# Output projections of a two-block fp32 kernel: raw weights requested during the attentions, low halves on VectorE, waits by chunk

## The reference

```python
# first block: forgetting attention and sliding-window attention, each 8 heads of 64
y = jnp.concatenate([oa * silu(za), ob * silu(zb)], axis=-1) @ w_out[l]      # 2048x1024 @ 1024x1024
x = x + gate[:, None, :] * rms_norm(y, g_post[l])
# second block: sparse latent attention a (8 heads of 64) and a recurrence r (width 512)
a = a * jax.nn.silu(gate_a)
r = rms_norm_2(r, hgrn_norm_g[l]).reshape(B, E, HGRN_WIDTH) * jax.nn.silu(gate_h)
y = jnp.concatenate([a, r], axis=-1) @ w_out[l]
h = layer_norm(DN_ALPHA * h + y, ln_g[l], ln_b[l])
```

## Time and profile before

| | us |
|---|---|
| median of 3 runs (3675.43 to 3689.69) | 3686.92 |
| profiled execution | 3693.26 |
| its span | 3691.6 |
| TensorE busy (share of the span) | 3301.4 (89%) |
| VectorE busy | 2017.7 (55%) |
| ScalarE busy | 1407.1 (38%) |
| GpSimd busy | 928.1 (25%) |

### The profile page before, as it was taken

One profiled execution on the slowest core, in us unless ns is written; L12 is line 12 of the kernel. 1 busy time (PEld: TensorE's weight loads), 2 busy tenths in 40 slices (PEclk: granted clock), 3 DMA queues, 4 the chain that ended last, 5 costly groups with the idle time before them and its releaser, 6 DMA issues. The chain is left out here.

```text
span 3691.6 us, 43885 instructions
## 1 busy us (share of the span) xinstructions
PE 3301.4 (89%) x15793; PEld 2518.3 (68%) x15840; DVE 2017.7 (55%) x3687; ACT 1407.1 (38%) x2381; POOL 928.1 (25%) x850
## 2 busy tenths in 40 slices
PE   3899999899999996995789999997995999999698
PEld 3799888656666664874567887886773666666387
DVE  5211011366666666332289999965672555555366
ACT  4100001144444444111157999232553333333344
POOL 0111111355454461001321223534232112111100
PEclk9999999899999998997899999998997999999899
DMA  5231224565454422435211335454135324222343
GB/s 200 72 103 62 94 83 122 134 140 128 106 128 106 103 70 100 137 119 213 70 44 49 87 109 177 132 156 165 50 112 158 97 66 93 59 56 59 107 150 128
DMA packets 331914, 400.83 MB, mean 109 GB/s; under 512 B 100324, under 2 KB 249188, under 8 KB 319124
## 3 DMA queue, kind: packets, MB, share of 16 engines
q1 hardware_dynamic: 257624, 282.31, 27.4%
q10 hardware_dynamic: 67488, 78.03, 6.9%
q0 software_dynamic: 6592, 37.75, 3.6%
HBM read 265.39 MB, written 132.62 MB: 108 GB/s over the span
## 5 line engine op out<-in xcount | busy, mean ns | idle before, releaser
L2218 PE MATMUL f_pO<-f_PT,f_vv 128*128 128x512 f32 (+3 forms) x944 | 383.1, 488 | 22.3 <-ACT f_PT L2248 22.3
L2310 DVE TENSOR_REDUCE f_mxc<-f_pM 128x1 f32<-128x512 f32 (+2 forms) x448 | 240.1, 541 | 226.7 <-PE f_pM L2142 129.0
L2248 ACT ACTIVATE f_PT<-f_pS 128x512 f32<-128x512 f32 (+3 forms) x472 | 221.4, 472 | 354.7 <-PE f_pS L2181 175.5
L2315 DVE CUSTOM_DVE_ANT_0 n_junk<-n_pM,n_chosen 128x512 bf16<-128x512 f32 (+4 forms) x352 | 200.2, 571 | 274.2 <-PE n_pM L2148 138.7
L2660 PE MATMUL cbank<-hT_high,cw_hi 128*128 128x512 f32 x800 | 316.6, 396 | 31.1 <-POOL cw_lo L2613 25.4
L2850 DVE TENSOR_SCALAR_CACHE_REDUCE sharedI<-xI,TI 128x768 bf16<-128x768 f32 (+10 forms) x276 | 339.6, 1297 | 5.4 <-DVE TI L2855 5.2
L571 PE MATMUL p_bank<-hT_high,p_w_hi 128*128 128x512 f32 (+1 forms) x768 | 304.9, 397 | 31.9 <-POOL p_w_lo L537 26.3
L2248 ACT ACTIVATE n_PT<-n_pS 128x512 f32<-128x512 f32 (+4 forms) x352 | 177.4, 504 | 390.9 <-PE n_pS L2198 320.1
L2660 PE MATMUL cbank<-hT_low,cw_hi 128*128 128x512 f32 x800 | 313.7, 392 | 0.0
L2660 PE MATMUL cbank<-hT_high,cw_lo 128*128 128x512 f32 x800 | 313.6, 392 | 0.0
L2218 PE MATMUL n_pO<-n_PT,n_vv 128*128 128x512 f32 (+4 forms) x704 | 305.6, 515 | 3.9 <-issue 1.3
(11 more groups left out here) (419 smaller groups left out, 7454.9 us busy)
## 6 DMA issues: line engine op xcount, KB each, us to landing
cw_raw<-in_w_in_dram SPq DMA_DIRECT2D x50, 512.0 KB, 4.6
f_zz<-scratch_z ACTq DMA_DIRECT2D x128, 128.0 KB, 2.9
p_w_raw<-in_w_in_dram SPq DMA_DIRECT2D x23, 512.0 KB, 3.7
scratch_z<-p_stage ACTq DMA_DIRECT2D x32, 256.0 KB, 2.4
scratch_qk_high<-p_stage ACTq DMA_DIRECT2D x32, 256.0 KB, 2.6
scratch_qk_low<-p_stage_low ACTq DMA_DIRECT2D x32, 256.0 KB, 3.2
f_vv<-scratch_vf SPq DMA_DIRECT2D x16, 512.0 KB, 14.4
f_rq<-scratch_qkb POOLq DMA_DIRECT2D x32, 256.0 KB, 6.7
```

The source lines that it names most:

```text
L2218: pe.matmul(pO[:, B % 2, c0:c1], lhsT=vv[0:nk, b, kt, :], rhs=PT[0:nk, u % PR, c0:c1], start=(kt == 0 and not heads[h].local), stop=(heads ...
L2248: act.activation(PT[0:nk, u % PR, c0:c1], pS[0:nk, u % SR, c0:c1], ACT.Exp, scale=0.125).then_inc(s_ex, 1)
L2310: v.tensor_reduce(to, pM[:, n % 2, 0:wd], AX.X, ALU.max).then_inc(s_mx, 1)
L2315: v.tensor_tensor_reduce(junk[:, n % 2, 0:wd], pM[:, n % 2, 0:wd], chosen[:, at:at + wd], 1.0, 3.0 * NEG, ALU.add, ALU.max, accum_out=to). ...
```

## The change

Three edits, in both output stages.

1. A buffer `lent` lives across an attention and the output stage behind it (eight chunks in the first, four in the second). In the attention `cosT`, `sinT`, `rqs`, `rks` ("f_") or `rq` ("n_") are slices of it. Behind the store of the last head's first block SyncE waits until all heads are split (`s_part`) and asks for the raw weights into `lent`, one transfer for two chunks. In o1 that is all of them; in o2 chunks 0 to 3, and GpSimd asks for 4 to 7 in the stage, as before.
2. VectorE subtracts for all eight chunks. ScalarE and VectorE prepare three (`FEW`), run the phases of the turns -3 to -1, and then prepare the other five; SyncE asks for `gain` and `offset` at that same point.
3. TensorE waits for the low parts chunk by chunk inside the first half of tile 0.

```diff
+        MORE = DC - lent.shape[1]
+        more = m.sb(n_("wraw"), [P, MORE, D]) if MORE else None
...
+        AHEAD, BEHIND, FEW = 3, 1, 3
+        def skeleton(phases, between=None):
...
+            turns(range(-AHEAD, 0))
+            if between is not None:
+                between()
+            turns(range(0, NT + BEHIND))
+        def wraw(k):
+            return lent[:, k, :] if k < DC - MORE else more[:, k - (DC - MORE), :]
...
         def _(gp):
-            for k in range(0, DC, 2):
-                gp.dma_start(wraw[:, k:k + 2, :], w_out[0, k * P:(k + 2) * P, :].rearrange("(k p) n -> p k n", p=P)
-                             ).then_inc(s_w[k // 2], 16)
-            split_low(gp, 1)
+            for k in range(DC - MORE, DC, 2):
+                gp.dma_start(more[:, k - (DC - MORE):k - (DC - MORE) + 2, :],
+                             w_out[0, k * P:(k + 2) * P, :].rearrange("(k p) n -> p k n", p=P)).then_inc(s_w[k // 2], 16)
...
                     for k in range(DC):
+                        if n == 0 and z == 0:
+                            pe.wait_ge(s_wl, k + 1)
...
-            for z in range(2):
-                pe.wait_ge(s_wl[z], DC // 2)
             skeleton(((0, multiply),))
...
+            def weights_high(ks):
+                for k in ks:
+                    act.wait_ge(s_w[k // 2], 16)
+                    act.activation(w_hi[:, k, :], wraw(k), ACT.Copy).then_inc(s_wh, 1)
+            weights_high(range(FEW))
...
-            split_low(v, 0)
+            def weights_low(ks):
+                for k in ks:
+                    v.wait_ge(s_wh, k + 1)
+                    v.tensor_tensor(w_lo[:, k, :], wraw(k), w_hi[:, k, :].bitcast(F32), ALU.subtract).then_inc(s_wl, 1)
+            weights_low(range(FEW))
...
# stage_attend, SyncE, in the loop over blocks
+                if j == 0 and h == NH - 1:
+                    sp.wait_ge(s_part, 2 * (NH if rel is not None else len(local_no)))
+                    for to, src, loaded in ahead:
+                        sp.dma_start(to, src).then_inc(loaded, 16)
```

More of the change, by code:

```diff
@@ L748, with stage_out @@
 DN_ALPHA = 2.0 ** 0.25
-def stage_out(nc, used, tag, gated_T, part, gates, w_out, rows_in, rows_out, gate_row=None, ln=None):
+def stage_out(nc, used, tag, gated_T, part, gates, w_out, rows_in, rows_out, lent, s_lent, gate_row=None, ln=None):
     HW = D // 2
@@ L774, in stage_out @@
         pY = m.ps(n_("pY"), [P, 2, D])
[L776 to L777 removed]
+        s_w = s_lent + [m.sem(n_(f"w_loaded{i}")) for i in range(MORE // 2)]
+        s_wh, s_wl = m.sem(n_("w_high")), m.sem(n_("w_low"))
         s_c = m.sem(n_("vectors_loaded"))
@@ L807, in _, with load_vectors @@
         def _(sp):
-            if ln:
-                for dst, src in ((gain, ln[0]), (offset, ln[1])):
-                    sp.dma_start(dst[:], src.to_broadcast([P, D])).then_inc(s_c, 16)
+            def load_vectors():
+                if ln:
+                    for dst, src in ((gain, ln[0]), (offset, ln[1])):
+                        sp.dma_start(dst[:], src.to_broadcast([P, D])).then_inc(s_c, 16)
             def load_parts(n, b, r):
@@ L897, in finish @@
                 act.activation(std[:, b:b + 1], var[:, b:b + 1], ACT.Sqrt).then_inc(s_std, 1)
-            skeleton(((1, high), (-1, finish)) + (((2, gate),) if part is not None else ()))
+            skeleton(((1, high), (-1, finish)) + (((2, gate),) if part is not None else ()), lambda: weights_high(range(FEW, DC)))
         @block.vector
@@ L929, in finish @@
                 one = slice(b, b + 1)
+                if ln and n == 0:
+                    v.wait_ge(s_c, 32)
                 v.wait_ge(s_st[b], r * 16)
@@ L954, in finish @@
                     v.tensor_tensor(tt[:, b, :], tt[:, b, :], xg[:, b, :], ALU.add).then_inc(s_res[b], 1)
-            if ln:
-                v.wait_ge(s_c, 32)
-            skeleton(((1, low), (-1, finish)) + (((2, gate),) if part is not None else ()))
+            skeleton(((1, low), (-1, finish)) + (((2, gate),) if part is not None else ()), lambda: weights_low(range(FEW, DC)))
 def stage_turn(nc, used, rows, meta, blocks, hT_meta, HT):
@@ L2914, in scratch, with lent_weights @@
         return nc.dram_tensor("scratch_" + name, shape, dt, kind="Internal").ap()
+    def lent_weights(w, to, sems):
+        return [(to[:, 2 * i:2 * i + 2, :], w[0, 2 * i * P:(2 * i + 2) * P, :].rearrange("(k p) n -> p k n", p=P), sem)
+                for i, sem in enumerate(sems)]
     HALF = SCRATCH_ROW
@@ L2958, in build_program @@
         heads += [local(H - 2), local(H - 1)]
-        stage_attend(nc, used, "f_", heads, 3, turns=turns, sinks=sinks)
-        stage_out(nc, used, "o1_", GT, None, None, w_out, x[0], X1, gate_row=gate_row)
+        m = Memory(nc, first, used)
+        lent, s_lent = m.sb("lent1", [P, DC, D]), [m.sem(f"o1_w_lent{i}") for i in range(DC // 2)]
+        stage_attend(nc, used, "f_", heads, 3, lent, lent_weights(w_out, lent, s_lent), turns=turns, sinks=sinks)
+        stage_out(nc, used, "o1_", GT, None, None, w_out, x[0], X1, lent, s_lent, gate_row=gate_row)
     clear(nc, used)
@@ L3003, in latent @@
                     k=[rows_of(t, h) for t in KTs])
-    stage_attend(nc, used, "n_", [latent(h) for h in range(H)], 2, rel=(MK, MKT, BV, BVT))
-    stage_out(nc, used, "o2_", GA2, RRT, GHT, w_out_2, X1, out[0], ln=(ln_g, ln_b))
+    with ExitStack() as last:
+        m = Memory(nc, last, used)
+        lent, s_lent = m.sb("lent2", [P, DC // 2, D]), [m.sem(f"o2_w_lent{i}") for i in range(DC // 4)]
+        stage_attend(nc, used, "n_", [latent(h) for h in range(H)], 2, lent, lent_weights(w_out_2, lent, s_lent),
+                     rel=(MK, MKT, BV, BVT))
+        stage_out(nc, used, "o2_", GA2, RRT, GHT, w_out_2, X1, out[0], lent, s_lent, ln=(ln_g, ln_b))
 INPUTS = ["x", "c", "positions", "w_ada", "b_ada", "g_pre", "w_in", "b_fgate", "sinks", "w_out", "g_post",
```

22 lines of the change are left out of this document (5 added, 17 removed).

## The result

| | before | changed |
|---|---|---|
| median, us | 3686.92 (3675.43 to 3689.69) | 3659.60 (3656.68 to 3664.95) |
| profiled execution (span) | 3693.26 (3691.6) | 3664.95 (3663.2) |
| TensorE idle before the two first matmuls | 32.7 + 34.0 | 14.5 + 23.8 |

The ratio is 0.9934, with a 95% interval of 0.9915 to 0.9952: 27.3 us faster, 18 to 31 by the interval. The forecast was 3659.

The account below looks back on a forecast made before the run. TensorE bounds both output stages behind holes of 32.75 and 33.97 us before their first matmuls. Gains of 16.2 (18.4 - 2.2) in o1 and 12.0 in o2 sum to 28.2 us, from 3686.92 to 3659; range 3646 to 3673.

Parts of the forecast that it names:

- The start of o1: First output stage: first matmul 6.7 us behind SyncE's first transfer instead of 25.1, a gain of 18.4 us.
- The end of the attention: Before o1: VectorE's last product waits for a store queued behind the early weights, costing 2.2 us, ends 0 and 8.5.
- The gate load's own term: Last attention block: ScalarE's gate load delayed 1.3 to 2.6 us by the weights, beside the store's 2.2.
- 5.2 us bound from the 7.9 us row: Upper delay of the last gate load, from loads landing in 7.9 to 8.4 us beside GpSimd's raw query loads.
- the rule that the prediction quoted: DMA engines take packets from queues in turn: each gate-load packet waits for one weight packet, 1.3 us in all.
- The start of o2: Second output stage: turned part lands at S + 11.1, first matmul at S + 13.9 instead of 26.7; gain 12.0 after waits.
- The cover of the other five chunks: In o1 the last five subtractions hide under the first tile's matmuls; without that cover they would cost 6.3 us.
- The chunk waits in o2: First tile of o2: TensorE waits some 0.8 us for chunks prepared behind the first three.
- Rival 1: Attention pays in full, 8.5 us instead of 2.2, and o2 gives 10: gain 19.9, time 3667; chance 16%.
- Rival 2: Clock stays at 1.2 GHz in both first tiles, costing 6.8 us in each stage: time 3672; chance 8%.
- Rivals 3 and 4: 3: the hole does not shrink, about 3680, 6%. 4: weights hold up the attention's end, slower, 3699 at 80 GB/s, 4%.

Follow-up runs that it names:

- p1: The changed kernel with the odd chunks' low-part subtractions given back to GpSimd; ratio 0.9935 to the kernel before.
- x1: The changed kernel with the first output stage's weights asked for two heads earlier in the attention; ratio 0.9912 to the kernel before.
- r1: The changed kernel with all eight chunks prepared ahead of the first tile's split; ratio 0.9962 to the kernel before.
- x5: The changed kernel with o2's chunks 4 to 7 asked for by SyncE behind the first tile's parts, not by GpSimd; ratio 0.9901 to the kernel before.
- r2: The changed kernel with TensorE waiting for all eight low parts, not chunk by chunk; ratio 0.9967 to the kernel before.
- z1: The changed kernel with the attention's weight request one block later, behind the last gate load; ratio 0.9927 to the kernel before.

## Why the prediction was right, and where its terms were off

**The start of o1: right.** S + 6.44 against S + 6.7, by the chain that was named: three copies, the turned part, high part, three subtractions, low part. ScalarE's first copy starts at S, and all subtractions are VectorE's. In the profile of p1, where GpSimd subtracts for one of the three, the start is nearly the same (S + 6.80).

**The end of the attention: the right wait, mis-sized.** Forecast 2.2 us, measured 4.8 (A), and 4.2 in the repeated profile. The mechanism held: VectorE's last product waited for the store that stands behind the weights, and the gate load's delay lay beside that wait and not on top. The term that failed is the landing of this store. It was put at 1451.3 on the clock of before, 14.4 us behind the head's first store, from 4.6 MB at 387 GB/s; it came after 16.9 us (16.3 in the repeated profile), because the queue moved 339 GB/s in the mean. x1 shows that the whole price goes when the request is early. The gate load's own term was too small as well: 1.3 to 2.6 us were named and ScalarE waited 4.7 (3.3 in the repeated profile), close to the 5.2 us bound from the 7.9 us row. By the rule that the prediction quoted from the Trainium skill ("DMA: Bandwidth & Descriptors", section "Queues, rings and completion order") the two loads should have landed 1.3 us later than before; they landed 4.0 and 4.7 us later, and the measurement decides against that use of it. This miss cost nothing, since the store landed later still.

**The start of o2: mis-sized.** Forecast S + 13.9, measured S + 16.59, all of it in the landing of the turned part: S + 14.06 instead of S + 11.1. The failed step is "with 1.7 of start the last of them lands at S + 11.1", and in it the rate, not the bytes: in r1 the same 3.41 MB, with nothing asked for behind them, were down at S + 13.7. The sum let them move at 330 and 387 GB/s from S + 1.7 on without a break; r1 shows a stretch of 2 us at 178 GB/s near the start and 2.6 us at 113 before the landing. Why the queues ran like this is not settled. The Trainium skill, "DMA: Bandwidth & Descriptors", section "Why a DMA increments its semaphore by 16 and not by 1", says that the engines of one transfer finish independently, and that only the full count means landed. The last row of r1 fits that, with the 16 engines busy for 0.39 of the time, but no run shows the engines one by one. The rest of the chain was right: 2.5 us from landing to matmul against 2.8. x5 shows that the part lands 7 us sooner without the weights beside it.

**The cover of the other five chunks: about right.** 6.3 us were named as its worth in o1; r1 gave 5.0 and r2 5.6. The chunk waits in o2 were put at 0.8; the trace has 0.2 of them, and D grew by 0.4.

**The rivals.** Rival 1 (gate load in full and the stores on top, 8.5) did not come: the gate load's delay was nearly as large as it said, but the stores' lay beside it, so that A grew by 4.8. For o2 it had the better number, 10, against 9.7 measured and 12 forecast. Rival 2 did not come in the changed kernel, where half clock lasted 5.8 and 3.3 us of the first tiles, not 15; p1 shows that a longer wait does take the clock back. Rivals 3 and 4 did not come; the last of the 4.19 MB landed 15.4 us after the first request, not 39.8.

**The sum.** The steps gave 28.2 and the touched stretches 23.6: 2.6 less at the attention's end, 2.7 less at the start of o2, 0.3 more at that of o1 and 0.4 more in the chunk waits. That the total still came out is not all owed to the steps: of the 28.4 us between the two profiled spans, 2.5 lie in the untouched middle and 2.3 ahead of A. The repeated comparison of medians gave 26.6, and with an interval of 18 to 31 us neither 23.6 nor 28.2 can be excluded. The number was right, and two of its four terms were not; that 3659 met 3659.60 so closely is luck.

## What to carry to other kernels

A prefetch into dead memory is not free beside small transfers that somebody waits for. Put it more than the time of its landing (here 4.19 MB, the last part 12.6 us after its issue) ahead of the last waits of a stage; x1 did, and paid nothing. At a stage's start, ask for what the first tile needs first, and for bulk behind it, on the same queue if need be; that alone was worth 5 to 7 us in C here. A forecast of a landing as bytes over the rate of a full queue came out 2.5 us too short at the end of the attention and 3.0 in o2, since the flow starts slowly and thins out at its end. Take the time from issue to landing of a like burst where a trace has one.

## What the runs showed of the hardware

- A gate load of 128 KB on ScalarE's queue, issued 0.7 to 1.2 us behind a request of 4.19 MB on SyncE's, landed after 6.8 to 8.3 us (5.4 and 6.4 in the repeated profile) instead of 2.8 to 3.6, although it is in another queue.
- A 64 KB store behind those weights landed after 11.5 us instead of 2.1, the last ones of z1 after 6.2.
- In r1 3.41 MB in two queues, 1.31 of them in packets of 512 B, took until S + 13.7. Only 6.0 us of that ran at 372 GB/s; ahead of them 2 us ran at 178, and the last 2.6 at 113 with the engines busy for 0.39 of the time.
- TensorE at full clock waited 2.28 us for data (o2 of p1) and went on at half clock for about 3.2 us; behind a wait of 1.25 us (o1 of p1) it did not.
- GpSimd's and VectorE's subtractions of two operands in on-chip memory slow each other: 128x1024 took up to 3.36 and 3.40 us, where the shortest took 2.44 and 1.22 (p1).
